# Shifted copies of the gated convolution input: issued half by SP and half by ScalarE

## The chip, the cores and the metric

The kernel runs on one core of a Trainium2 chip. The metric is the device time of one execution in microseconds (us); the median of several executions counts. One further execution of each kernel was taken with the hardware profiler, and all rows of the trace are of that one.

## The reference

Two layers of an encoder, run over 512 prompt tokens and 64 sample tokens with the same weights. Each layer has a mixer (sparse attention beside a Conformer convolution) and a hierarchical mixture of experts. The part that matters here is the convolution, over 512 channels and with width 31:

```python
a, b = jnp.split(u, 2, axis=-1)
g = a * jax.nn.sigmoid(b)
...
padded = jnp.concatenate([conv_past, g], axis=1)
y = lax.conv_general_dilated(padded, conv_w.astype(g.dtype)[:, None, :], window_strides=(1,),
                             padding='VALID', dimension_numbers=('NWC', 'WIO', 'NWC'),
                             feature_group_count=D_CONV) + conv_b
y = jax.nn.silu(layer_norm(y, ln_conv_g, ln_conv_b))
```

`u` is a part of the layer's input projection; `conv_past` is zero for the prompt and 30 cached rows for the sample. Attention, projections, experts and norms are all computed too; the change doesn't touch them.

## The kernel before

Everything is float32. Each engine runs its own program, and semaphores order them. The 512 channels of the convolution are four blocks of 128, i = 0 to 3, worked on in each of the two layers:

- TensorE computes the two halves of a block's projection (`u_block(i)`: 64 matmuls, 448 prompt tokens and then the other 128).
- ScalarE takes the sigmoid of one half (`gates(i)`, L1197 and L1199), writing into gT; VectorE multiplies it by the other half (L1613, L1614) and raises `s_glu`. VectorE does this between rounds of the top-k selection (L1543, L1544).
- The taps are applied by matmuls with a contraction over 128 partitions that hold 4 shifts of 32 channels. For this the gated block gT has to be copied four times with a shift: `shifted(i)` (L412 to L420) issues 16 SBUF to SBUF transfers of 32 partitions x 634 numbers (79 KB), for shift j = 0 to 3 and channel group g = 0 to 3. They go to G4[i % 2], so block i waits (`s_conv`) until the convolution of block i - 2 has been done. Each transfer raises `s_g4[i % 2]` by 16.
- TensorE runs `conv(i)` (L695, 128 matmuls in two banks) when all 256 counts of the block are there, GpSimd's matrix of taps (`tap_matrix`, L1934) is ready, and the banks were emptied by ScalarE's `conv_out(i - 1)` (L1205).

TensorE's order is u_block(0), u_block(1), conv(0), u_block(2), conv(1), u_block(3), conv(2), some transposes (L531), conv(3). In layer 0 parts of a modulation product (`ada3`, L551) lie between them. The order of the work is written out by hand on every engine.

SP issues all weight loads (`load`, L397) in program order; each waits until TensorE has freed its slot of W (`w_free`). In layer 0 the blocks' `shifted` calls stand among loads of `w_ada`; in layer 1 all four stand behind two loads of `w_out`, and further loads of `w_out` and of the experts' weights follow. ScalarE issues stores and a few small loads on its own queue: those of this stage are the new convolution state (L1217, L1218), after `conv_out(2)`. Behind them it copies transposed keys into kT (L1222) and then runs `conv_out(3)`.

After the convolution come the layer norm over channels, the attention's logits and outputs, the output projection (L844), the routing and the experts (the matmuls at L508, with x_d rows fetched by SP at L463 and results stored by ScalarE at L1333).

Of the kernel before, what the change touches and what calls it, by code (L numbers as in the profile page):

```python
# [101 lines left out]
def program(nc, A, O):  # L102
    ctx = ExitStack()
    with ctx:
# [3 lines left out]
        def sem(name):  # L108
            return ctx.enter_context(nc.semaphore(name))
# [34 lines left out]
        def part(at, n, *shape):  # L144
            v = arena[:, at:at + n]
            if len(shape) == 2:
                return v.rearrange("p (a b) -> p a b", a=shape[0])
            if len(shape) == 3:
                return v.rearrange("p (a b c) -> p a b c", a=shape[0], b=shape[1])
            return v  # L150
# [7 lines left out]
        gT = part(10880, 4 * GW, 4, GW)  # L158
# [4 lines left out]
        G4 = [part(0, 4 * GS, 4, GS), part(19760, 4 * GS, 4, GS)]  # L163
# [47 lines left out]
        s_glu, s_conv = sem("s_glu"), sem("s_conv")  # L211
        s_g4 = [sem(f"s_g4{i}") for i in range(2)]
# [30 lines left out]
        def leave(eng, name):  # L243

            eng.drain().then_inc(arrived, 1)
            eng.wait_ge(go[name], 1)
            eng.sem_clear(go[name])
# [17 lines left out]
        def mixer_use(l, c, hf):  # L265

            if l == 1:
                return MIX1 + 2 * c + hf
            return (MIX0, MIX0 + 2, U_Q, U_U0, U_U1, U_OUT0, U_OUT0 + 2)[c] + hf
# [6 lines left out]
        def ada3_use(k):  # L276

            return U_ADA3A + k if k < 2 else U_ADA3B + k - 2

        def expert_use(l, e):  # L280

            return (EXP0, EXP1)[l] + 3 * e
# [20 lines left out]
        def tail_of(i):  # L303

            at = 10880 + GW * i + 30 + UHEAD
            return arena[:, at:at + 188].rearrange("p (a c) -> p a c", a=2)[:, :, 0:DEC]

        def u_tail(i, ab):

            at = 2 * P * (i % 2) + P * ab  # L310
            return ps[7][:, at:at + P].rearrange("p (a c) -> p a c", a=2)
# [75 lines left out]
        def _(sp):  # L387
# [3 lines left out]
            def load(use, src):  # L391
                slot, turn = use % 6, use // 6
                if turn > 0:
                    sp.wait_ge(w_free[slot], turn)
                n = src.shape[-1] * src.shape[-2]
                dst = W[:, slot, 0:n].rearrange("p (k c) -> p k c", c=src.shape[-1])
                sp.dma_start(dst, src).then_inc(w_ld[slot], 16)  # L397
# [6 lines left out]
            def ada(first_use, third, ks=range(KC)):  # L404
                l, q = THIRDS[third]
                for k in ks:
                    load(first_use + k, wada[l, :, k:k + 1, 2048 * q:2048 * q + 2048])
# [3 lines left out]
            for l in range(DEPTH):  # L411
                def shifted(i):  # L412

                    sp.wait_ge(s_glu, 4 * l + i + 1)
                    if i >= 2:
                        sp.wait_ge(s_conv, 4 * l + i - 1)
                    for j in range(4):
                        for g in range(4):
                            sp.dma_start(G4[i % 2][32 * j:32 * j + 32, g, 0:634],  # L419
                                         gT[32 * g:32 * g + 32, i, j:j + 634]).then_inc(s_g4[i % 2], 16)  # L420

                def narrow(hf):

                    use = mixer_use(l, 1, hf)
                    if use // 6 > 0:
                        sp.wait_ge(w_free[use % 6], use // 6)
                    rows = W[:, use % 6, 0:4 * NARROW].rearrange("p (k c) -> p k c", c=NARROW)
                    for at, c0, c1 in ((0, CK, CIQ), (256, CIK, CU)):
                        sp.dma_start(rows[:, :, at:at + c1 - c0], win[l, :, 4 * hf:4 * hf + 4, c0:c1]).then_inc(w_ld[use % 6], 16)

                for c in range(7):
                    if l == 0 and c == 2:
                        ada(U_ADA1, 0)
                        ada(U_ADA2, 1)
                    for hf in range(2):
                        ks = slice(4 * hf, 4 * hf + 4)
                        if c == 1:
                            narrow(hf)
                        elif c in (3, 4):
                            c0 = CU + 512 * hf + 256 * (c - 3)  # L440
                            load(mixer_use(l, c, hf), win[l, :, :, c0:c0 + 256])
                        else:
                            w, c0, c1 = {0: (win, CIQ, CIK), 2: (win, CQ, CK), 5: (wout, 0, 512), 6: (wout, 512, 1024)}[c]
                            load(mixer_use(l, c, hf), w[l, :, ks, c0:c1])
                    if l == 0 and c == 3:
                        ada(ada3_use(0), 2, range(2))
                    if l == 0 and c == 4:
                        shifted(0)
                        ada(ada3_use(2) - 2, 2, range(2, 6))
                        shifted(1)  # L450
                        shifted(2)
                        ada(ada3_use(2) - 2, 2, range(6, KC))
                        shifted(3)
                        ada(U_ADA4, 3)
                        ada(U_ADA5, 4)
                    if l == 1 and c == 5:
                        for i in range(4):
                            shifted(i)
                def rows(e):

                    if e >= 3:
                        sp.wait_ge(L["tx"], 2 * (e - 1))
                    sp.dma_start(xg[:, e % 2, :], x_d[e * P:e * P + P, :]).then_inc(s_xg[e % 2], 16)  # L463

                for e in range(NE):
                    for j, w in enumerate(wexp):
                        load(expert_use(l, e) + j, w[l, e])
                        if j == 1 and 2 <= e < NE - 1:
                            rows(e + 1)
                    if e == 1:  # L470
                        sp.wait_ge(s_xs, (l + 1) * 160)
                        rows(1)
                        rows(2)

                sp.wait_ge(n_cnt, l + 1)
                sp.reg_load(further, jobs[0:1, XJ:XJ + 1])
                with sp.If_ne(further, 0):
                    sp.wait_ge(L["tx"], 2 * NE)
                    sp.wait_ge(s_xo[l], 160)
                    with sp.Fori(0, sp.snap(further, min_val=0, max_val=XJ)) as x:  # L480
                        sp.dma_start(xg[:, 0, :], x_d[bass.ds(x * P + XROW, P), :]).then_inc(M["jld"], 16)
                        sp.reg_load(expert, jobs[0:1, bass.ds(x, 1)])
                        e = sp.snap(expert, min_val=0, max_val=NE - 1)
                        for s, w in enumerate(wexp):
                            sp.dma_start(JW[s].rearrange("p (k c) -> p k c", c=D if s == 2 else DE),
                                         w[l, bass.ds(e, 1)].rearrange("e p k f -> (e p) k f")).then_inc(M["jld"], 16)
                        leave(sp, "sp")
# [503 lines left out]
        def _(act):  # L991
# [40 lines left out]
            for l in range(DEPTH):  # L1032
# [129 lines left out]
                for n, (t, h) in enumerate((t, h) for t in SCORED for h in range(8)):  # L1162
# [11 lines left out]
                    g = n // 4  # L1174
# [19 lines left out]
                def gates(i):  # L1194

                    act.wait_ge(L["uproj"], 4 * i + 2)
                    S.activation(gT[:, i, 30:30 + UHEAD], ps[4 + 2 * (i % 2)][:, 0:UHEAD], ACT.Sigmoid)  # L1197
                    act.wait_ge(L["uproj"], 4 * i + 4)
                    S.activation(tail_of(i), u_tail(i, 1), ACT.Sigmoid).then_inc(L["sig"], 1)  # L1199

                def conv_out(i):

                    act.wait_ge(s_conv, 4 * l + i + 1)
                    for b, (d, n) in enumerate(((0, SEQ), (SEQ, DEC))):
                        ins = S.activation(cy[:, i, d:d + n], ps[b][:, 0:n], ACT.Identity, bias=vT[:, 40 + i:41 + i])  # L1205
                    ins.then_inc(L["cyd"], 1)

                gates(0)
                for i in range(1, 4):
                    gates(i)  # L1210
                    conv_out(i - 1)

                for n in range(2):
# [811 lines left out]
```

## Time and profile before

| | us |
|---|---|
| median of 3 runs | 1380.69 |
| lowest and highest of them | 1379.9, 1380.77 |
| the profiled execution | 1378.88 |
| its span, first to last instruction | 1377.0 |

Busy shares of the span: TensorE 87%, VectorE 43%, ScalarE 24%, GpSimd 11%. The mean granted TensorE clock is 0.943 of full speed. The DMA engines move 206 GB/s in the mean. TensorE is busy most of the time, but a busy share doesn't tell what a change in one stage is worth: for that, look at where TensorE stands idle in that stage, and at what ended each wait. The chain that ended last is followed back from the last instruction, each time to what released it. Its names with a q (SPq) are sequencers: time in which an engine issues a transfer.

### The profile page before, as it was taken

To read this page: it belongs to the slowest core of one execution; us is meant where nothing else is said; L and a number is where in the kernel's file an instruction comes from. 1 tells how busy PE (TensorE), PEld (TensorE's weight loads), DVE (VectorE), ACT (ScalarE), POOL (GpSimd) and SP (SyncE) were. 2 spreads that over 40 slices of the span, in tenths; PEclk is the share of its full clock that TensorE was granted. 3 is DMA by queue.
4 is the path that set the end of the run, shared out by engine and by line. 5 is a ranking of instruction groups with operands and counts; after the bars stand their busy time and mean duration, and the time that the engine had idled before them with its cause. 6 is when DMAs were issued, how large, how long until landed. Compare 5 with 4: busy or idle time off the path is not lost.

```text
span 1377.0 us, 16342 instructions
## 1 busy us (share of the span) xinstructions
PE 1197.3 (87%) x6331; PEld 719.1 (52%) x6331; DVE 594.9 (43%) x1496; ACT 330.2 (24%) x779; POOL 153.1 (11%) x218
## 2 busy tenths in 40 slices
PE   4898996996999898999954989999888989999990
PEld 0462353543545586777732544554445558777760
DVE  1327899004546631111105538993265664111115
ACT  2224210024542111111103333101266111111111
POOL 0312150001000151000002112300100011000002
PEclk9999998998999989999985999999799998999995
DMA  9528999280780479999937220223303046899976
GB/s 362 158 66 325 363 329 285 52 285 4 269 304 31 156 205 386 369 363 366 350 140 262 62 75 0 81 66 79 124 26 60 31 149 210 276 363 365 363 268 221
DMA packets 136888, 283.96 MB, mean 206 GB/s; under 512 B 11582, under 2 KB 91878, under 8 KB 130410
## 3 DMA queue, kind: packets, MB, share of 16 engines
q1 hardware_dynamic: 116128, 208.66, 45.4%
q0 software_dynamic: 8352, 42.50, 8.9%
q10 hardware_dynamic: 12329, 31.74, 6.6%
q8 instruction: 51, 0.84, 0.3%
q14 instruction: 28, 0.22, 0.1%
HBM read 236.86 MB, written 52.40 MB: 210 GB/s over the span
## 4 chain that ended last, share of the span: by engine, by line
PE 65%; DVE 15%; DMA 9%; SPq 3%; ACT 3%; issue 3%; ACTq 0%; POOLq 0%; POOL 0%; DVEq 0%
PE ps L508 39%; PE ps L844 7%; PE ps L531 6%; PE ps L695 4%; SPq L419 3%; DVE arena L1544 3%; DVE small L1543 2%; DMA X<-in_x_sample 2%; PE ps L759 2%; PE ps L896 2%; DMA W<-in_w_gate 2%; PE ps L809 2%; DVE arena L1585 2%; DMA W<-in_w_up 2%; PE ps L551 1%
## 5 line engine op out<-in xcount | busy, mean ns | idle before, releaser
L508 PE MATMUL ps<-W,arena 128*128 128x256 f32 (+1 forms) x1280 | 347.4, 427 | 9.4 <-DMA W<-in_w_up 4.9
L508 PEld LDWEIGHTS ps<-W,arena 128*128 128x128 f32 x1280 | 241.6, 193 | 84.2 <-issue 49.1
L508 PE MATMUL ps<-W,hT 128*128 128x512 f32 (+1 forms) x384 | 156.5, 565 | 3.1 <-ACT hT L1052 3.1
L531 PE MATMUL ps<-C,arena 128*128 128x128 f32 (+3 forms) x795 | 114.2, 281 | 47.3 <-DVE arena L1463 18.0
L531 PEld LDWEIGHTS ps<-C,arena 128*128 128x128 f32 (+3 forms) x795 | 91.3, 144 | 88.1 <-issue 35.6
L844 PE MATMUL ps<-W,hT 128*128 128x512 f32 (+1 forms) x384 | 129.7, 534 | 1.2 <-DMA W<-in_w_out 1.2
L508 PE MATMUL ps<-hT,W 128*128 128x128 f32 (+1 forms) x512 | 126.6, 408 | 0.0
L508 PEld LDWEIGHTS ps<-W,hT 128*128 128x128 f32 x384 | 74.3, 197 | 77.4 <-issue 62.7
L1868 DVE TENSOR_TENSOR arena<-arena,ps 128x256 f32<-128x256 f32 x32 | 13.5, 421 | 219.0 <-ACT arena L1338 219.0
L508 PEld LDWEIGHTS ps<-hT,W 128*128 128x128 f32 x512 | 77.8, 191 | 49.6 <-issue 49.2
L844 PEld LDWEIGHTS ps<-W,hT 128*128 128x128 f32 (+1 forms) x384 | 56.7, 175 | 62.7 <-issue 59.2
L695 PE MATMUL ps<-arena 128*32 128x64 f32 (+1 forms) x1024 | 68.3, 425 | 19.6 <-DMA arena<-arena 19.6
L1543 DVE MAX8 small<-arena 64x8 f32<-64x576 f32 (+3 forms) x132 | 80.5, 610 | 3.7
L1544 DVE MATCH_REPLACE8 arena<-small,arena 64x576 f32<-64x576 f32 (+3 forms) x132 | 78.5, 594 | 0.0
L551 PE MATMUL ps<-W,scT 128*32 128x512 f32 x384 | 58.6, 709 | 9.9 <-DMA W<-in_w_ada 9.5
L1963 POOL DMA_INDIRECT x_d<-arena,sid x30 | 29.1, 970 | 330.8 <-DVE sid L1775 324.7
L1991 POOL DMA_INDIRECT arena<-y_d,sid x20 | 19.3, 967 | 400.5 <-DVEq L256 202.6
L1863 DVE COPY arena<-ps 128x512 f32<-128x512 f32 x32 | 22.1, 692 | 93.5 <-PE ps L508 93.5
L1338 ACT ACTIVATE arena<-ps 128x256 f32<-128x256 f32 x32 | 12.3, 384 | 194.6 <-PE ps L508 187.5
L695 PEld LDWEIGHTS ps<-arena 128*32 128x32 f32 x1024 | 24.9, 112 | 64.7 <-issue 43.5
L759 PE MATMUL ps<-arena 64*128 64x128 f32 (+3 forms) x128 | 37.0, 509 | 16.8 <-DVE small L1636 16.2
L1666 DVE COPY arena<-ps 128x512 f32<-128x512 f32 (+1 forms) x50 | 32.8, 687 | 38.3 <-PE ps L531 37.9
(263 smaller groups left out, 1202.8 us busy)
## 6 DMA issues: line engine op xcount, KB each, us to landing
W<-in_w_ada SPq DMA_DIRECT2D x48, 1024.0 KB, 6.8
W<-in_w_gate SPq DMA_DIRECT2D x32, 1024.0 KB, 10.2
W<-in_w_up SPq DMA_DIRECT2D x32, 1024.0 KB
W<-in_w_down SPq DMA_DIRECT2D x32, 1024.0 KB, 8.0
y_d<-arena ACTq DMA_DIRECT2D x33, 512.0 KB, 7.4
W<-in_w_in SPq DMA_DIRECT2D x16, 1024.0 KB, 7.5
arena<-x_d SPq DMA_DIRECT2D x31, 512.0 KB, 11.3
arena<-arena SPq DMA_DIRECT2D x128, 79.2 KB, 2.1
```

What stands on the lines that cost most here:

```text
L419: sp.dma_start(G4[i % 2][32 * j:32 * j + 32, g, 0:634], gT[32 * g:32 * g + 32, i, j:j + 634]).then_inc(s_g4[i % 2], 16)
L508: ins = T.matmul(out, l, r, start=n == 0, stop=n == len(pairs) - 1, skip_group_check=True)
L531: count(T.transpose(o, i, ident[0:m, 0:m]), done if n == len(outs_ins) - 1 else None)
L551: ins = T.matmul(out[32 * j:32 * j + 32, :], scT[:, k, :], W[:, use % 6, 512 * j:512 * j + 512], start=k == 0, stop=k == KC - 1, skip_grou ...
L695: ins = T.matmul(ps[b][32 * g:32 * g + 32, 0:n], W4[:, i % 2, NQ * g + q, :], G4[i % 2][:, g, s0 + 4 * q:s0 + 4 * q + n], start=q == 0, st ...
L759: ins = T.matmul(ps[logit_bank(job)][:, 0:b - a], qT[hp, i, tokens(t)], kT[1][hp, a:b], start=True, stop=True)
L809: ins = T.matmul(ps[6 + n % 2][64 * a:64 * a + 64, q * P:(q + 1) * P], v, heads, start=c == 0, stop=c == last, skip_group_check=True)
L844: ins = T.matmul(ps[5 + n % 3][64 * side:64 * side + rows_of(t), 0:c1 - c0], hT[:, 4 * q + k, tokens(t)], wv[:, k, c0:c1], start=q == 0 an ...
L1543: chain(V.max(m8, sc))
L1544: chain(V.match_replace(sc, m8, sc, MARK))
L1666: V.tensor_copy(pT[0:kn, c, :], ps[4 + job % 2][0:kn, :]).then_inc(L["pta"], 1)
L1963: G.indirect_dma_start(out=x_d[:, :], out_offset=bass.IndirectOffsetOnAxis(ap=table[0:m, 5 * k + t:5 * k + t + 1], axis=0), in_=HR[0:m, t, ...
```

## The change

Of the four shifts, SP now issues j = 0 and 1. ScalarE issues j = 2 and 3, with the same two waits ahead of them, in its program: block 0 right after `gates(0)`, and blocks 1 to 3 each between `gates(i)` and `conv_out(i - 1)`. Transfers, buffers, semaphores and counts are the same.

```diff
@@ SP
                     sp.wait_ge(s_glu, 4 * l + i + 1)
                     if i >= 2:
                         sp.wait_ge(s_conv, 4 * l + i - 1)
-                    for j in range(4):
+                    for j in range(2):
                         for g in range(4):
                             sp.dma_start(G4[i % 2][32 * j:32 * j + 32, g, 0:634],
                                          gT[32 * g:32 * g + 32, i, j:j + 634]).then_inc(s_g4[i % 2], 16)
@@ ScalarE
+                def shifted(i):
+
+                    act.wait_ge(s_glu, 4 * l + i + 1)
+                    if i >= 2:
+                        act.wait_ge(s_conv, 4 * l + i - 1)
+                    for j in range(2, 4):
+                        for g in range(4):
+                            act.dma_start(G4[i % 2][32 * j:32 * j + 32, g, 0:634],
+                                          gT[32 * g:32 * g + 32, i, j:j + 634]).then_inc(s_g4[i % 2], 16)
+
                 gates(0)
+                shifted(0)
                 for i in range(1, 4):
                     gates(i)
+                    shifted(i)
                     conv_out(i - 1)
```

## Rows read from the trace of the kernel before

**Rows 1.** The page: its span, and the chain that ended last, by line.

```profile
span 1377.0 us, 16342 instructions
...
PE ps L508 39%; PE ps L844 7%; PE ps L531 6%; PE ps L695 4%; SPq L419 3%; DVE arena L1544 3%; DVE small L1543 2%; DMA X<-in_x_sample 2%; PE ps L759 2%; PE ps L896 2%; DMA W<-in_w_gate 2%; PE ps L809 2%; DVE arena L1585 2%; DMA W<-in_w_up 2%
```

**Rows 2.** One line, L419: durations (min/median/max ns), and who waited (us, times).

```profile
L419 SPq DMA_DIRECT2D arena<-arena x128: 507/591/4056, 209.5 to 962.6; - x128
...
  PE ps L695: 19.6, 4
```

**Rows 3.** TensorE's timeline, layer 0: start us, us, operation [idle before <-releaser].

```profile
228.93 9.89 PE L695 MATMUL ps<-arena 128*32 128x512 f32 x128 [10.45 <-DMA arena<-arena]
...
294.83 7.97 PE L695 MATMUL ps<-arena 128*32 128x512 f32 x128 [2.28 <-DMA arena<-arena]
```

**Rows 4.** TensorE's timeline, layer 1, the four convolutions' stretch.

```profile
903.84 7.97 PE L695 MATMUL ps<-arena 128*32 128x512 f32 x128 [3.39 <-DMA arena<-arena]
911.74 15.87 PE L508 MATMUL ps<-hT,W 128*128 128x448 f32 x64
...
960.45 0.80 PE L531 MATMUL ps<-C,arena 128*128 128x128 f32 x5
964.73 10.63 PE L695 MATMUL ps<-arena 128*32 128x512 f32 x128 [3.48 <-DMA arena<-arena]
```

**Rows 5.** SP's timeline, block 3 of layer 0 and of layer 1.

```profile
281.48 11.47 SPq L419 DMA_DIRECT2D arena<-arena  x16
...
952.57 10.59 SPq L419 DMA_DIRECT2D arena<-arena  x16
```

**Rows 6.** The chain in order of time (start us, us, what): block 0, layer 0.

```profile
209.51 4.06 SPq L419
...
222.48 6.40 DMA arena<-arena
```

**Rows 7.** The chain in order of time: blocks 0 and 3, layer 1.

```profile
891.11 0.55 SPq L419
...
899.31 1.75 SPq L419
...
901.73 2.07 DMA arena<-arena
...
961.30 0.59 SPq L419
...
961.94 0.59 SPq L419
```

**Rows 8.** The timeline of all engines near 961 us: ScalarE's two stores.

```profile
961.24 0.59 ACTq L1217 DMA_DIRECT2D out_new_conv_prompt<-crows  x1
961.87 0.35 ACTq L1218 DMA_DIRECT2D out_new_conv_sample<-crows  x1
```

**Rows 9.** DMA packets in two windows, 218.0 to 222.6 and 225.4 to 227.9.

```profile
DMA packets 532, 0.85 MB, mean 185 GB/s; under 512 B 156, under 2 KB 225, under 8 KB 532
...
DMA packets 148, 0.98 MB, mean 390 GB/s; under 512 B 20, under 2 KB 20, under 8 KB 33
```

**Rows 10.** Windows: busy of PE, PEld, DVE, ACT, POOL; PEclk, DMA share, GB/s.

```profile
218.00:222.60 4.60, 0.47 (x8) 0.00 (x0) 4.33 (x13) 0.00 (x0) 0.00 (x0) 1.00 1.01 185
...
891.00:902.30 11.30, 9.45 (x48) 6.39 (x46) 10.82 (x23) 0.82 (x2) 0.00 (x0) 1.00 0.43 102
...
903.84:911.80 7.96, 7.96 (x129) 3.08 (x129) 7.58 (x20) 0.00 (x0) 0.00 (x0) 1.00 0.25 61
964.73:975.30 10.57, 10.57 (x129) 3.38 (x129) 0.00 (x0) 0.00 (x0) 0.00 (x0) 0.74 1.03 354
```

**Rows 11.** ScalarE's timeline, layer 1: sigmoid of block 1, `conv_out(2)`.

```profile
896.92 0.54 ACT L1197 ACTIVATE arena<-ps 128x448 f32<-128x448 f32 x1 [11.75 <-PE ps L508]
...
959.27 0.89 ACT L1205 ACTIVATE arena<-ps,vT 128x512 f32<-128x512 f32 x2 [7.65 <-PE ps L695]
```

**Rows 12.** The chain in order of time, further on: a wait for a weight load.

```profile
390.29 9.63 DMA W<-in_w_out
```

## The prediction

> **What bounds the kernel now.** I read the page first: TensorE has the largest part of the chain that ended last, and the lines of the chain name one that is no arithmetic at all, SP's issue of the shifted copies (L419), with 3% [rows 1]. The view of that one line then says how the 3% comes about: 128 issues with a median of 0.59 us, and TensorE stood idle four times, 19.6 us in all, until their data had landed [rows 2]. TensorE's own timeline places the four: in layer 0 before the convolution of block 0 (10.45 us) and of block 3 (2.28 us) [rows 3], in layer 1 before that of block 0 (3.39 us) and of block 3 (3.48 us) [rows 4]. Before the convolutions of blocks 1 and 2 there is no idle time, since 15.8 us of the next block's products lie between [rows 4]. So only four of the eight copied blocks can give anything, and at most what TensorE waits for them.
>
> The four waits aren't alike. In layer 1, block 0, the chain holds SP's issues one after the other from 891.11 on, nearly all of 0.59 us with 0.04 between, one of 1.75 us, and then 2.07 us until the last one has landed [rows 7]: issue bounds it. Block 3 of both layers is the same, 11.47 us and 10.59 us for sixteen issues [rows 5]. In layer 0, block 0, the first issue alone took 4.06 us, and from the start of the last one until all had landed passed 6.40 us [rows 6]. There the DMA engines are full: in the 4.6 us before 222.6 their share is 1.01 [rows 10], and in that stretch 69 packets of 1 KB (225 under 2 KB less 156 under 512 B), the rest of weight loads queued earlier, still move among the copies. From 225.4 to 227.9 only 13 packets of copies are left (33 less 20), one every 0.19 us, while 115 larger ones pass [rows 9]. I read this as one DMA engine that is behind with earlier loads and does its whole share of the block last. This is an inference; the trace doesn't name a packet's engine here.
>
> **The change, part by part.** Per block SP gives up eight issues (j = 2, 3) and ScalarE takes them, behind the same two waits. The same sixteen transfers move the same bytes and raise the same semaphore to the same count.
>
> *Issue.* Eight issues at a pitch of 0.63 us are 5.07 us instead of 10.1 us, on each queue. Does ScalarE's pitch hold, and does SP's, when both issue? The trace has one place where they do. At 961.24 and 961.87 ScalarE issued two stores of 30 rows (0.59 and 0.35 us) [rows 8] while SP's copies went on with 0.59 us each [rows 7]: four issues in 1.3 us where SP alone makes two. So I take 0.63 us for both. The bounds are 0.35 us and the longest of the undisturbed chain, 1.75 us.
>
> The Trainium skill has a rule against this change: "Perfetto Trace Analysis", section "DMA Instruction — HWDGE (DVE, Sync)", says that the two issuing sequencers share one descriptor generator, which is locked for exclusive use while it makes a transfer's descriptors. The rows of the double issue show SP's duration unaltered, so if there is such a lock, it covered only a part of the 0.59 us there.
>
> *The engines that carry the copies.* With SP alone their share is 0.43 over layer 1's block 0 [rows 10]. Twice the rate asks for 0.86: it fits, with some queueing. I leave the 2.07 us from the last issue to landing as it is and allow 1 us more.
>
> *Layer 1, block 0.* The copies begin at 891.11. Eight issues (5.07), one long one (1.16 over the normal, as in rows 7) and 2.07 end at 899.4. TensorE is free at 903.84 - 3.39 = 900.45. The wait is gone with 1.0 us to spare: 3.39 us gained, and what is late next is TensorE itself. An issue may cost up to 0.76 us before any of it comes back.
>
> *Layer 1, block 3.* The copies begin at 952.57, 3.4 us earlier then, at 949.2, if the product of VectorE moves up with TensorE's work; its rounds of the selection could hold it back. They land at 949.2 + 5.07 + 0.6 + 2.1 = 957.0; TensorE ends its transposes at 961.25 - 3.39 = 957.9 [rows 4]. Gained 3.48 us. A second gain hangs on it: this convolution took 10.6 us at a granted clock of 0.74, where the one of block 0 took 7.96 us at 1.00 [rows 10]. The clock fell to its lower level, 1.2 GHz, while TensorE stood idle behind a few transposes. Without the idle time I expect the 7.97 us: 2.66 us more. In layer 0 the shorter wait of 2.28 us cost no clock (7.97 us [rows 3]).
>
> *Layer 0, block 3.* The copies begin at 281.48 [rows 5]; 5.07 + 1.4 (11.47 less sixteen pitches) + 2.5 (from the last issue, at 292.36, to TensorE's start at 294.83) end at 290.5. TensorE is free at 294.83 - 2.28 = 292.55 [rows 3]. Gained 2.28 us.
>
> *Layer 0, block 0.* Here I take nothing. If one engine does its share of 32 pieces last, its work is the same by whichever queue the pieces come; ScalarE's half only mixes with the old loads instead of standing behind them. Bounds: the whole wait of 10.45 us plus the slow part of the convolution behind it (9.89 against 7.97, 1.92) gained; on the other side, SP reaches its next weight loads, and ScalarE its half of block 1, some us earlier than SP does now, both before the last pieces have moved. Some ten pieces then take 0.19 instead of 0.10 us and up to eight get a neighbour of 0.19: 1 + 1.5 = 2.5 us lost.
>
> The Trainium skill, "DMA: Bandwidth & Descriptors", section "Queues, rings and completion order", says that a DMA engine serves the queues in turn, packet by packet. By that, ScalarE's half overtakes old loads but the engine's total stays; it agrees with taking nothing, and no row here shows the turns themselves.
>
> *ScalarE.* It gets 64 issues, 5.1 us per block, at nothing. They lie ahead of the sigmoids or the evacuation (`conv_out`) of the block before. In its timeline ScalarE is idle 11.75 us before the sigmoids of block 1 and 7.65 us before the last `conv_out` [rows 11]. Where the wait for VectorE's product ends late, `conv_out` may come late by up to the eight issues, 5 us; its reader, the next convolution, starts 15.8 us after the end of the one that it evacuates [rows 4]. Without that cover each late `conv_out` would cost its delay. Also moved past: SP's loads behind each block start about 5 us earlier, and ScalarE's two stores of the convolution state and the three copies to kT stand behind block 3, which is issued by 954.3, before they can start.
>
> *Sum.* 3.39 + 3.48 + 2.66 + 2.28 + 0 = 11.8 us. Further on the chain goes through TensorE and through weight loads that are issued when TensorE frees a slot [rows 12], so the gain is passed on. The profiled execution took 1378.88 us (span 1377.0 and 1.9 around it), 1.8 us under the median of the runs: 1367.1 on its scale, 1380.69 - 11.8 = 1368.9 on that of the median.
>
> **The rivals.**
> *The two issues take turns.* If the generator is held for the whole 0.59 us, sixteen issues take as long on two queues as on one, and the kernel stays at 1380.7. This is the rule of the lock in its strict form. Against it: rows 7 and 8. For it: those stores go to HBM and are but two. The gain begins to fall when a pair of issues takes over 0.76 us per queue and is gone near 1.4. The same time results if the split does nothing because the copies are bound by the engines that carry them; against that, the share of 0.43. Chance 0.10.
> *Layer 0's block 0 is helped as well.* ScalarE's half doesn't stand behind SP's first issue of 4.06 us nor in SP's queue of old loads. With half of the wait gone, 5 us, the time is 1364. For it: the order of the queues; against it: a full engine. Chance 0.13.
> *The clock doesn't come back* in layer 1's block 3, or falls elsewhere for as long: 9.15 us gained, 1371.5. Chance 0.10.
> *Slower: handing over costs more than it saves.* If two engines issuing at once make each issue as long as the longest seen, 1.75 us, eight take 14 us and land at 891.1 + 14 + 2.1 = 907.2, against 903.8: 3.4 us lost at each of four places, 13.6 us, 1394. It decides from 1.33 us per issue (8 x 1.33 + 2.07 = the 12.7 us of now). Only single rows are that long. Chance 0.05.
> *My forecast*, 1368.9, with the small losses in layer 0's block 0: chance 0.62.
>
> **How the numbers follow.** Within 0.2% is 1377.9 to 1383.5 (about what a measurement can tell from no change). Faster: forecast, helped block, clock, 0.85; within: the turns, 0.10; slower 0.05. The forecast with its bounds runs from 1366 to 1372.5. The range takes in the helped block at 1364 and, above, the lost clock plus a loss of 2.5 us and part of a slower pitch: 1376. What is left out is the turns, the slower case and the far end of the helped block, under 0.2.
>
> **What would show it.** The line of the copies 64 times on SP and 64 times on ScalarE, medians near 0.59 us; no idle time of TensorE before three of the four convolutions; layer 1's last convolution at 8 us with a clock near 1; and still some 10 us before layer 0's first. I am wrong if the medians come near 1.2 us, if landing takes 4 us more, if a wait for ScalarE's `conv_out` or the sigmoids appears before a convolution, or if the clock falls at a new place.

## The result, and the profile after

| | before | after |
|---|---|---|
| median of the runs, us | 1380.3 (1377.57 to 1380.77, 4 runs) | 1363.78 (1356.02 to 1367.84, 4 runs) |
| profiled execution, us | 1378.88 | 1367.84 |
| its span, us | 1377.0 | 1365.9 |

The ratio is 0.989, with a 95% interval of 0.985 to 0.992: faster, at the lower end of the forecast range, near the 1364 us of the rival in which layer 0's block 0 is helped too. A second measurement of the changed kernel, below, gave 1365.96 us and a ratio of 0.991 (0.989 to 0.993). Which waits went decides between the two, not the time. The profiled execution was the slowest of its four, so the 11.0 us by which the two profiled executions differ are less than the medians' 16.5.

The page of the changed kernel, the rows that answer to [rows 1]:

```profile
span 1365.9 us, 16346 instructions
...
PE ps L508 43%; PE ps L844 7%; PE ps L531 6%; PE ps L695 5%; DVE arena L1556 2%; DVE small L1555 2%; DMA X<-in_x_sample 2%; PE ps L759 2%; PE ps L896 2%; DMA W<-in_w_up 2%; PE ps L809 2%; PE ps L551 1%; DVE arena L1597 1%; PE ps L520 1%; PE ps L650 1%
```

SP's issue, 3% of the chain before, is no longer among the lines. The two lines of the copies (min/median/max ns), and who waited for them, as in [rows 2]:

```profile
L419 SPq DMA_DIRECT2D arena<-arena x64: 507/593/2778, 209.3 to 949.7; - x64
...
  PE ps L695: 8.4, 1
...
L1215 ACTq DMA_DIRECT2D arena<-arena x64: 514/614/2275, 209.3 to 950.0; - x64
```

One wait is left of four. The medians are 0.593 and 0.614 us with both queues at work, against 0.591 for SP alone. TensorE's timeline of the changed kernel, the rows that answer to [rows 3] and [rows 4]:

```profile
226.80 10.85 PE L695 MATMUL ps<-arena 128*32 128x512 f32 x128 [8.39 <-DMA arena<-arena]
...
291.31 7.97 PE L695 MATMUL ps<-arena 128*32 128x512 f32 x128
...
896.59 7.97 PE L695 MATMUL ps<-arena 128*32 128x512 f32 x128
...
953.93 7.97 PE L695 MATMUL ps<-arena 128*32 128x512 f32 x128
```

Three convolutions start without idle time. The last one takes 7.97 us where it took 10.63. The first one still waits, and the chain in order of time says for what:

```profile
209.26 2.78 SPq L419
...
216.13 10.63 DMA arena<-arena
```

SP's last copy is issued at 216.1 instead of 222.5 [rows 6], and yet the block has landed only at 226.8: issue doesn't bind it. ScalarE's timeline in layer 1, block 1, as the nearest it came to harm:

```profile
903.34 7.28 ACTq L1215 DMA_DIRECT2D arena<-arena  x8
910.67 0.89 ACT L1205 ACTIVATE arena<-ps,vT 128x512 f32<-128x512 f32 x2 [13.70 <-issue]
```

The convolution whose output is evacuated here ends at 904.5 (896.59 + 7.97), so `conv_out(0)` comes 6.1 us late, 1 us more than the 5 us allowed for, since these eight issues took 7.28 us. The next convolution starts at 920.3 without idle time.

### The profile page after: what moved, and what is told of

Its sections match the earlier page's. It is cut to its first block, busy times and chain, and to the rows that moved or that the text cites. A ratio compares the mean times of both kernels' runs of the same rounds, so it can differ in the third digit from the quotient of the medians.

```text
span 1365.9 us, 16346 instructions
## 1 busy us (share of the span) xinstructions
PE 1198.7 (88%) x6331; PEld 720.3 (53%) x6331; DVE 594.5 (44%) x1496; ACT 330.5 (24%) x779; POOL 152.7 (11%) x218
## 4 chain that ended last, share of the span: by engine, by line
PE 71%; DVE 14%; DMA 7%; ACT 3%; issue 2%; SPq 1%; ACTq 0%; POOLq 0%; POOL 0%; DVEq 0%
PE ps L508 43%; PE ps L844 7%; PE ps L531 6%; PE ps L695 5%; DVE arena L1556 2%; DVE small L1555 2%; DMA X<-in_x_sample 2%; PE ps L759 2%; PE ps L896 2%; DMA W<-in_w_up 2%; PE ps L809 2%; PE ps L551 1%; DVE arena L1597 1%; PE ps L520 1%; PE ps L650 1%
## 5 line engine op out<-in xcount | busy, mean ns | idle before, releaser
L1880 DVE TENSOR_TENSOR arena<-arena,ps 128x256 f32<-128x256 f32 x32 | 13.5, 421 | 219.2 <-ACT arena L1350 219.2
L695 PE MATMUL ps<-arena 128*32 128x64 f32 (+1 forms) x1024 | 66.6, 418 | 8.4 <-DMA arena<-arena 8.4
L695 PEld LDWEIGHTS ps<-arena 128*32 128x32 f32 x1024 | 24.7, 111 | 51.8 <-issue 42.0
L650 PE MATMUL ps<-arena 64*64 64x512 f32 (+3 forms) x128 | 44.1, 614 | 8.0 <-ACT arena L1168 8.0
## 6 DMA issues: line engine op xcount, KB each, us to landing
W<-in_w_gate SPq DMA_DIRECT2D x32, 1024.0 KB, 10.5
```

The source lines that it names most:

```text
L650: count(T.matmul(ps[5 + n % 3][0:rows_of(t), 0:b - a], q, kT[0][hp, a:b], start=True, stop=True), L["dots"])
L695: ins = T.matmul(ps[b][32 * g:32 * g + 32, 0:n], W4[:, i % 2, NQ * g + q, :], G4[i % 2][:, g, s0 + 4 * q:s0 + 4 * q + n], start=q == 0, st ...
```

## The experiments

My theory: three waits are issue time, which halves, and the first block of layer 0 is bound by transfers. The rivals: the two issuing queues take turns; or the gain has to do with what follows the copies in SP's queue. TensorE's convolutions stand at L695 in all kernels but one, where the line is L692.

**The changed kernel again.**

> The changed kernel once more, unaltered, for the spread of its times and for a second trace. My theory (the waits for issue are gone at three places, the first block of layer 0 is held by transfers): 1364 us, within 4. In the trace the copies' line stands 64 times on SP and 64 times on ScalarE with medians of 0.59 to 0.62 us, TensorE has no idle time before the convolutions of block 3 in layer 0 and of blocks 0 and 3 in layer 1, and 7 to 10 us before block 0 of layer 0. If the first result was a lucky one, the time is over 1372.

1365.96 us (1363.13 to 1368.46, 6 runs); ratio 0.991 (0.989 to 0.993). In its trace the first convolution waits 7.71 us and no other waits. The result stands, and so does the reason: the helped block asked for half of the 10.45 us, and 8.39 and 7.71 us are left.

**The split in one layer alone.** `shifted` of ScalarE returns at once in the other layer, where SP issues all sixteen:

```diff
-                    for j in range(2):
+                    for j in range(2 if l == 1 else 4):
@@ ScalarE, shifted(i)
+                    if not (l == 1):
+                        return
```

> The split in layer 1 alone; in layer 0 SP issues all sixteen copies of a block. My theory: 3.39 + 3.48 us of waits and 2.66 us of low clock go, 9.5 us under the kernel before, about 1371 (1368 to 1374). TensorE waits about 10 us and 2.3 us in layer 0 as before. Rival (the two issuing queues take turns, and the gain of the change comes from SP's loads being issued earlier in layer 0): at most 2 us under the kernel before, with issues of about 1.2 us.

1367.1 us, ratio 0.993 (0.991 to 0.995); the rival's 2 us at most are excluded. The time is 0.9 us under the expected 1368 to 1374. In the trace the steps of layer 1 make 9.7 us, as expected; TensorE is 7.0 us ahead of the kernel before when it comes to them, though nothing was changed up to there. TensorE's timeline of this kernel: both waits of layer 1 are gone (893.40 and 950.74, without idle time). In layer 0, with SP issuing as before, it reads

```profile
225.40 9.70 PE L695 MATMUL ps<-arena 128*32 128x512 f32 x128 [7.22 <-DMA arena<-arena]
...
290.50 7.97 PE L695 MATMUL ps<-arena 128*32 128x512 f32 x128 [1.67 <-DMA arena<-arena]
```

> The split in layer 0 alone. My theory: the 2.28 us before block 3 go; block 0 gives between -1 and 3 us, since transfers and not issues hold it: 1375 to 1379. Rival (ScalarE's half overtakes the loads in SP's queue and shortens block 0 by half of its 10.45 us): 1371 to 1374, with an idle time of at most 5 us before the first convolution.

1374.59 us, ratio 0.997 (0.996 to 0.999), between the expectation (1375 to 1379) and the rival (1371 to 1374). The rival also asked for a first wait of at most 5 us, and that is not so. The timeline:

```profile
226.57 10.16 PE L695 MATMUL ps<-arena 128*32 128x512 f32 x128 [7.04 <-DMA arena<-arena]
...
291.07 7.97 PE L695 MATMUL ps<-arena 128*32 128x512 f32 x128 [0.61 <-DMA arena<-arena]
...
896.07 9.66 PE L695 MATMUL ps<-arena 128*32 128x512 f32 x128 [3.16 <-DMA arena<-arena]
...
958.86 10.94 PE L695 MATMUL ps<-arena 128*32 128x512 f32 x128 [3.69 <-DMA arena<-arena]
```

The two layers add up within the noise (about 10 and 4 us by the ratios against 12.4 by that of the second measurement of the whole). The first convolution waits 7.22 us with SP alone and 7.04 us with the split: no gain of the change shows there. Before block 3 of layer 0, SP alone waits 1.67 us in the one trace and 2.28 in [rows 3], and the split still waits 0.61 us here, so in that place the split is worth 1.1 to 2.3 us. The first wait differs from execution to execution: it was 10.45 us in [rows 3], and 10.41 us with three shifts on SP, below. Layer 1's last convolution again takes nearly 11 us when it waits 3.69 us.

**Three shifts to one.** SP issues j = 0 to 2, ScalarE j = 3.

> SP issues shifts 0 to 2 (twelve copies per block), ScalarE shift 3 alone (four). My theory (the wait is the longer queue's issue time): twelve issues at 0.63 us are 7.6 us. Layer 1, block 0: the copies end 2.5 us later than with eight, 1 to 2 us after TensorE is free; block 3 likewise 1 to 2 us; layer 0, block 3 between 0 and 1.5 us. 2 to 5 us slower than the even split: 1367 to 1371. Rival (the two queues take turns on one generator and only the total of sixteen counts): no difference from the even split.

1367.38 us, ratio 0.992 (0.988 to 0.995): by time not to be told from the even split. The trace decides:

```profile
295.75 7.97 PE L695 MATMUL ps<-arena 128*32 128x512 f32 x128 [1.74 <-DMA arena<-arena]
...
899.87 7.97 PE L695 MATMUL ps<-arena 128*32 128x512 f32 x128 [1.76 <-DMA arena<-arena]
...
958.86 7.97 PE L695 MATMUL ps<-arena 128*32 128x512 f32 x128 [1.58 <-DMA arena<-arena]
```

In layer 1 the waits are 1.76 and 1.58 us, where the even split has none and SP alone 3.16 to 3.69 in the traces so far: the longer queue sets the landing, as expected. In layer 0 the 1.74 us tell nothing, since SP alone waited 1.67 to 2.28 us there; expected were 0 to 1.5. The clock differs too: with 1.58 us of idle time layer 1's last convolution takes 7.97 us, with 3.69 us it takes 10.94.

**All sixteen on ScalarE, none on SP.**

> ScalarE issues all sixteen copies of a block, SP none. My theory: the longer queue has sixteen issues of 0.61 us again, so the waits of 3.4, 3.5 and 2.3 us come back: 1376 to 1382, as the kernel before, and ScalarE's evacuations come up to 10 us late without anybody waiting for them. Rival (the gain comes from SP's queue being free for its weight loads, or from ScalarE's queue being served ahead of SP's): most of the gain stays, 1364 to 1370.

1404.6 us, ratio 1.019 (1.015 to 1.023). Both theories missed this: it is 25 us slower than SP alone, although ScalarE's median issue is 0.612 us. TensorE's timeline:

```profile
233.84 9.51 PE L695 MATMUL ps<-arena 128*32 128x512 f32 x128 [14.88 <-DMA arena<-arena]
...
312.74 9.32 PE L695 MATMUL ps<-arena 128*32 128x512 f32 x128 [15.65 <-DMA arena<-arena]
...
922.16 9.66 PE L695 MATMUL ps<-arena 128*32 128x512 f32 x128 [3.30 <-DMA arena<-arena]
...
989.91 10.35 PE L695 MATMUL ps<-arena 128*32 128x512 f32 x128 [8.65 <-DMA arena<-arena]
```

ScalarE has issued block 3 of layer 0 by 296.3, but the block lands at 312.7. What else is moving is in the DMA view of 285.5 to 297:

```profile
q1 hardware_dynamic: 482, 3.56, 88.7%
q10 hardware_dynamic: 250, 0.44, 12.4%
...
W<-in_w_ada SPq DMA_DIRECT2D x6, 1024.0 KB, 14.2
arena<-arena ACTq DMA_DIRECT2D x16, 79.2 KB, 11.6
```

SP, with no copies to issue, goes straight on to its weight loads; those move 3.56 MB while the copies move 0.44. In program order SP's own copies had kept these loads back. The test is to give SP a wait where its copies stood:

```diff
                     if i >= 2:
                         sp.wait_ge(s_conv, 4 * l + i - 1)
+                    sp.wait_ge(s_g4[i % 2], (2 * l + i // 2 + 1) * 256)
```

> ScalarE issues all sixteen copies of a block, and SP, where its own copies stood, waits until that block's copies have landed (s_g4) before it goes on with its loads. The run without that wait took 1404.6 us instead of the 1376 to 1382 that I had expected, with TensorE waiting 14.9, 15.7, 3.3 and 8.7 us. New theory: SP's copies also held back SP's own weight loads, and without them six loads of 1 MB run beside the copies (layer 0, block 3: landing 16 us after issue). Then this kernel has waits of 3 to 4 us again before block 3 in both layers and the time is 1376 to 1384. Rival (a copy issued by ScalarE costs more, or ScalarE's late evacuations hold TensorE): it stays over 1398.

1378.33 us, ratio 0.998 (0.997 to 1.000), against 1404.6 without the wait. TensorE waits 8.03, 1.36, 3.75 and 4.30 us, near those of SP alone (the 1.36 before block 3 of layer 0 is under the expected 3 to 4):

```profile
291.19 7.97 PE L692 MATMUL ps<-arena 128*32 128x512 f32 x128 [1.36 <-DMA arena<-arena]
...
967.74 9.27 PE L692 MATMUL ps<-arena 128*32 128x512 f32 x128 [4.30 <-DMA arena<-arena]
```

So the 26 us came from SP's loads running beside the copies. Issued by ScalarE the copies cost no more time than issued by SP, and no convolution waits for ScalarE's late evacuations.

**What holds the first block of layer 0.** The DMA view of the kernel before, 160 to 205 us, just ahead of it:

```profile
q0 software_dynamic: 269, 14.48, 94.5%
q1 hardware_dynamic: 197, 0.69, 5.2%
...
W<-in_w_in SPq DMA_DIRECT2D x2, 1024.0 KB, 34.3
```

GpSimd's queue (q0) moves 14.48 MB of its four copies into x_d and y_d, in packets of 54 KB in the mean; SP's queue moves 0.69 MB. SP issues two loads of 1 MB at 182.6 and 185.9; by this view they take 34.3 us to land (the trace has the landing of the first alone), and they stand ahead of the copies. Between 187 and 205, when all three queues have work, the view shows how they share:

```profile
q0 software_dynamic: 109, 6.09, 100.8%
q1 hardware_dynamic: 109, 0.11, 2.7%
q10 hardware_dynamic: 109, 0.06, 1.0%
```

Each queue moves 109 packets (q10 is ScalarE's), and the bytes are 6.09, 0.11 and 0.06 MB.

First I moved all four behind the squares for the layer norm, with the split:

```diff
-                if l == 0:
-                    pool.wait_ge(L["rel"], 32)
-                    for n in range(3):
-                        pool.dma_start(x_d[n * D:n * D + D, :], A["w_out"][0]).then_inc(s_fill, 16)
-                    pool.dma_start(y_d[XROW:SPARE, :], A["w_out"][0]).then_inc(s_fill, 16)
@@ behind the product into sqc
+                if l == 0:
+                    for n in range(3):
+                        pool.dma_start(x_d[n * D:n * D + D, :], A["w_out"][0]).then_inc(s_fill, 16)
+                    pool.dma_start(y_d[XROW:SPARE, :], A["w_out"][0]).then_inc(s_fill, 16)
```

> The changed kernel, and GpSimd's four large copies into x_d and y_d (L1949, L1950 before) are issued in layer 0 after the squares for the layer norm instead of before the queries' rope, some 120 us later. My theory: those copies (GpSimd's queue moves 210 to 370 GB/s from 155 to 209 us, and SP's queue 3 to 8 GB/s meanwhile) hold two weight loads back until 209 us, and these then stand ahead of layer 0's first block. Without them the 8.4 us of idle time and the 2.9 us of low clock before and in the first convolution go: 1352 to 1355. Against it: the copies collide with loads at 320 to 360 us, which may give 5 us back. Rival (the copies' own pieces or the loads behind them hold the engines): the idle time before the first convolution stays over 6 us and the time near 1364.

1371.09 us, ratio 0.995 (0.993 to 0.997), where 1352 to 1355 was expected. The mechanism is confirmed and the time isn't: the first convolution starts without idle time and takes 7.95 us,

```profile
216.39 7.95 PE L695 MATMUL ps<-arena 128*32 128x512 f32 x128
```

and at 343 us TensorE is 17 us ahead of the kernel before, but at 400 only 0.4 us. Of this, 13.1 us are waits for loads (waits of that stretch: us in total, times, longest), where the changed kernel waits 0.3 us for them:

```profile
PE ps L551 <- DMA W<-in_w_ada: 10.7, 5, 4.6
PE ps L844 <- DMA W<-in_w_out: 2.4, 2, 1.8
```

From 343 to 360 GpSimd's queue moves 3.15 MB of the moved copies beside SP's 1.73.

Next the four were spread, one each behind tap_matrix(2) and tap_matrix(3), two behind the squares, once with SP alone and once with the split.

> The kernel before (SP issues all copies), with GpSimd's four large copies into x_d and y_d issued where the DMA engines are nearly idle: one each behind tap_matrix(2) and tap_matrix(3), two behind the squares for the layer norm. My theory: without the large copies ahead of it, layer 0's block 0 is bound by issue like the others, 10.1 us and landing, of which TensorE waits about 3.5 us instead of 10.45, and its clock doesn't fall: 8 to 9 us under the kernel before, 1369 to 1372, if nothing is given back at 340 to 400 us as in the run with the late copies. Rival: the wait stays near 10 us.

> Both: the copies issued half by SP and half by ScalarE, and GpSimd's large copies spread. My theory: all four waits are gone and nothing is given back at 340 to 400 us: 11 to 14 us under the changed kernel, 1351 to 1355. In the trace TensorE has no idle time before any convolution. If the spread copies collide with the blocks 2 and 3, up to 5 us of it come back as waits before those convolutions.

1379.26 us, ratio 1.000 (0.998 to 1.002), and 1359.96 us, ratio 0.988 (0.984 to 0.991): both missed, 7 and 5 us above what was expected. With SP alone the first wait falls to 2.52 us, but layer 0 now also waits 5.30 us before block 1, where one of the spread copies (4.19 MB from 232 to 252 us) runs beside the block's own, and 2.80 before block 3. Both convolutions are slower after it (10.49 and 9.66 us). The gain that I expected went there. With the split, waits of 1.00, 1.90 and 2.20 us are left in layer 0. The last pair moves just one copy, that into y_d, behind the squares, and leaves three:

```diff
-                    pool.dma_start(y_d[XROW:SPARE, :], A["w_out"][0]).then_inc(s_fill, 16)
@@ behind the product into sqc
+                if l == 0:
+                    pool.dma_start(y_d[XROW:SPARE, :], A["w_out"][0]).then_inc(s_fill, 16)
```

> The kernel before (SP issues all copies), with only one of GpSimd's four large copies, the one into y_d, moved behind the squares for the layer norm; three stay. Theory: the three end 12 us earlier, near 197 us, and the two weight loads held back by them are done before 209 us. Layer 0's block 0 is bound by issue: TensorE waits 2.5 to 4 us instead of 7 to 10, its clock doesn't fall (2 us), and the one moved copy costs nothing, since the DMA engines are idle from 305 to 340 us: 6 to 9 us under the kernel before. Rival (the spread copies of the earlier runs helped only because all four were gone): 0 to 3 us.

> The same with the copies issued half by SP and half by ScalarE. Theory: no idle time of TensorE before any of the convolutions of layer 0, nothing given back at 340 to 400 us: 9 to 12 us under the changed kernel (1365), 1353 to 1356, and 3 to 6 us under the run with the spread copies (1360.0). Rival: the wait before the first convolution stays over 5 us, 1362 or more.

1373.23 us, ratio 0.995 (0.993 to 0.997), and 1354.35 us (1352.88 to 1355.55), ratio 0.982 (0.980 to 0.983). With SP alone the held loads now land after 21.1 us instead of 34.3, and the first convolution waits 2.48 us. That is issue, as the chain in order of time shows: issues one behind the other, and 2.07 us from the last to landing, where it was 6.40:

```profile
218.51 0.59 SPq L419
...
219.14 2.07 DMA arena<-arena
```

TensorE's timeline:

```profile
221.25 7.97 PE L695 MATMUL ps<-arena 128*32 128x512 f32 x128 [2.48 <-DMA arena<-arena]
```

With the split no convolution waits:

```profile
218.59 7.94 PE L695 MATMUL ps<-arena 128*32 128x512 f32 x128
...
280.38 7.97 PE L695 MATMUL ps<-arena 128*32 128x512 f32 x128
...
884.66 7.97 PE L695 MATMUL ps<-arena 128*32 128x512 f32 x128
...
942.00 7.97 PE L695 MATMUL ps<-arena 128*32 128x512 f32 x128
```

This version is faster than both kernels: 26.5 us under the kernel before, and 10 to 14 us under the changed one (whose two measurements gained 16.5 and 12.7). The Trainium skill, "DMA: Bandwidth & Descriptors", section "Queues, rings and completion order", says that a DMA engine takes a whole packet from each queue in turn. The trace agrees: 109 packets of each of three queues from 187 to 205 us, with bytes as 55 to 1 between q0 and q1.

## Why the prediction was right, and where it was off

**Issue.** Right for the typical copy. I took 0.63 us per copy on each queue, from two stores that overlapped SP's copies [rows 7, 8]. The median pitches are 0.64 us. The Trainium skill ("Perfetto Trace Analysis", "DMA Instruction — HWDGE (DVE, Sync)") has the generator locked only until the descriptors are made. A lock for the whole issue, which the rival assumed, doesn't show: durations rose by some hundredths of a microsecond. But a block's eight issues took from 4.97 to 7.46 us on a queue, not 5.07, because single issues are longer, and these come on both queues at the same moment (one of ScalarE's from 905.5 and one of SP's from 905.9, both until 907.8); the cause of these stays open. The chance for the slower rival hung on these becoming the rule, and they didn't. (The prediction names two points where the gain would be gone, 1.4 and 1.33 us per issue; its own sum gives 1.33.)

**Layer 1.** Right in all three terms. TensorE comes to this stage 3.79 us ahead of the kernel before and is 7.26 us ahead at the convolution of block 0, a gain of 3.47 where 3.39 was forecast; 10.81 us at that of block 3 (3.55 for 3.48); and 13.46 behind it (2.65 for 2.66, the clock). These lags compare the starts of the same matmuls in the two traces.

**Layer 0, block 3.** Right: 2.3 us between the two profiled executions (1.17 us ahead before, 3.52 after); against the other traces of SP alone, which waited 1.67 and 1.78 us here, it is less. The allowance of 2.5 us for landing was too short, since the copies now took 3.6 to 5.3 us from the end of an issue to landing, with SP's loads nearer behind; the last one landed at 290.8, half a microsecond before TensorE came to it at 291.3.

**Layer 0, block 0.** Right that it gives little: 2.1 us earlier, 1.0 of it lost in the convolution, which took 10.85 us instead of 9.89. Even the 2.1 us aren't shown to be the split's: with SP alone in layer 0 the same convolution started at 225.4, earlier than the changed kernel's 226.8. The reason was right only in part. "Loads queued earlier" it was, but what kept them queued, GpSimd's large packets, I had not looked for. With one of these copies moved away, SP alone has 2.07 us from its last issue to landing instead of 6.40. That one DMA engine is behind the others stays an inference.

**The sum.** 11.8 us forecast, 11.0 between the profiled executions. That they lie so close is in part luck: the 1.2 us of block 0 and 0.3 us on the way to layer 1, which the sum didn't have, and later losses of 3.1 us, which it didn't have either, partly cancel. TensorE is 13.5 us ahead at 976 us; 1.5 us of this went in the sums of the layer norm right behind, which took 7.47 us instead of 5.97, at a mean granted clock of 0.60 instead of 0.75, and 1.6 us more near 1126, where the mean granted clock is 0.83 (1110 to 1140) instead of 0.89 (1121 to 1151 before). So the clock also fell in a new place, one of the prediction's signs of being wrong, at a small price. The second trace lost 1.2 and 0.2 us there and ended 13.4 us ahead. The layer norm's row in the changed kernel:

```profile
977.64 7.47 PE L508 MATMUL ps<-arena,C 128*128 128x512 f32 x16 [1.02 <-ACT arena L1241]
```

The medians gained 16.5 and, measured again, 12.7 us. The runs of the changed kernel spread over 5 and 12 us in the two measurements and those of the kernel before over up to 17, and the part above 11.8 isn't explained by any row. The wait of the first block differed between 7.0 and 10.5 us among the traces that left GpSimd's copies in place and had copies on SP; it may be one source of the spread, which is not shown.

**The missing step.** I wrote that loads are issued 5 us earlier behind each block, and priced that at nothing or a little. In this change it is little. The run with all copies on ScalarE shows what the same effect costs when nothing is left on SP to hold the loads back: 26 us. That my sum held because SP kept half of the copies is likely, not shown: no run gave the split a wait that holds the loads back.

## What to carry to other kernels

A string of small transfers that somebody waits for is issue time, and a second queue halves it: look at the longer queue's count times its pitch against the reader's slack. A queue's program order also keeps later loads out of the way; when transfers leave a queue, ask what then starts beside them. And look at what fills the DMA engines just before a latency-critical block: a bulk copy with large packets on another queue held the loads issued behind it for 34 us here, and moving one such copy to an idle stretch gained about as much again as the split, while moving all four gained less when they were spread and cost time, against the split alone, when they were moved together.

## What the runs showed of the hardware

- Two queues issuing at once kept nearly their own pitch: 0.593 us on SP and 0.614 us on ScalarE per copy of 32 rows of 2.5 KB, against 0.591 alone.
- Beside packets of 54 KB on GpSimd's queue, SP's queue got 0.69 of 15.3 MB in 45 us. While three queues had work, each moved 109 packets in 18 us, whatever their size.
- TensorE ran the same 128 matmuls in 7.97 us after 0 to 1.9 us of idle time, and after more than 3 us mostly in 9.3 to 10.9 us, with a granted clock of 1.2 GHz for a part of them. Between 2 and 3 us both occurred, and in the kernel before layer 1's first convolution took 7.97 us after 3.39 us, so the length of the idle time alone doesn't decide it.
